# First block of a three-block fp32 kernel: the local projection in four halves between the dilated attention units, the gate sigmoids spread out, the score maxima taken piece by piece

## The reference, cut to what matters

```python
h = rms_norm(x, g_norm1) * (1.0 + sc1) + sh1
proj = h @ w_in
qa, ka, va, qb, kb, vb, gates = jnp.split(proj, split_at, axis=-1)
...
o_a = neighbourhood_attention(qa, ka, va, rpb)          # 8 heads, "local"
for g, (win, dil) in enumerate(DIL_CONFIGS):            # 3 groups of 4 heads, "dilated"
    o_g, lse_g = dilated_window_attention(qb[:, :, sl], kb[:, :, sl], vb[:, :, sl], win, dil)
...
wts = softmax(lse over the three groups);  o_b = sum over g of wts * o_g
gate_a, gate_b = split(sigmoid(gates + b_gate), 2)
merged = gate_a * (o_a @ w_proj_a) + gate_b * (o_b @ w_proj_b)
x = x + gt1 * (merged @ w_o)
```

## Time and profile before

| | us |
|---|---|
| median of 3 runs | 2222.18 (2220.04 to 2225.40) |
| the profiled execution, own time | 2223.02 |
| its span, first to last instruction | 2221.2 |
| PE busy | 2132.8 (96%) |
| DVE busy | 1329.5 (60%) |
| ACT busy | 1148.2 (52%) |
| POOL busy | 86.6 (4%) |
| mean granted TensorE clock | 0.986 of full |

### The profile page before, as it was taken

The page is one execution under the profiler, slowest core; times in us unless marked ns, Lnnn a source line. Parts: engine busy times, 40 slices in busy tenths (PEclk is TensorE's granted clock), DMA queues, the critical chain, the costliest instruction groups (busy, mean ns, idle before and its releaser), DMA issues. The chain is left out here.

```text
span 2221.2 us, 40757 instructions
## 1 busy us (share of the span) xinstructions
PE 2132.8 (96%) x15594; PEld 1865.5 (84%) x15594; DVE 1329.5 (60%) x1821; ACT 1148.2 (52%) x1697; POOL 86.6 (4%) x92
## 2 busy tenths in 40 slices
PE   7999889999999999989999999999999998999998
PEld 5787778887888998888998887887998897998887
DVE  3446375556556987566656555555897575756554
ACT  3454644445445566655445445445557664535444
POOL 1000000000000010100000000000002010000000
PEclk9999999999999999999999999999999999999999
DMA  9763245554553454421455554554354421345553
GB/s 375 279 236 110 77 154 183 187 184 172 189 188 144 179 180 143 154 94 58 171 186 185 188 188 170 189 189 171 136 187 155 163 102 54 137 181 180 189 189 123
DMA packets 53468, 373.16 MB, mean 168 GB/s; under 512 B 6320, under 2 KB 6448, under 8 KB 9424
## 3 DMA queue, kind: packets, MB, share of 16 engines
q1 hardware_dynamic: 47808, 342.00, 42.4%
q0 software_dynamic: 5520, 29.23, 3.8%
HBM read 370.10 MB, written 1.11 MB: 167 GB/s over the span
## 5 line engine op out<-in xcount | busy, mean ns | idle before, releaser
L1507 ACT ACTIVATE HI<-ring 128x1024 fp32r<-128x1024 f32 x606 | 626.3, 1056 | 738.1 <-PE banks L559 397.2
L2067 DVE TENSOR_TENSOR LO<-ring,HI 128x1024 fp32r<-128x1024 f32 x322 | 393.8, 1225 | 369.6 <-ACT HI L1507 369.3
L2073 DVE TENSOR_TENSOR LO<-ring,HI 128x2048 fp32r<-128x2048 f32 x135 | 309.6, 2294 | 242.0 <-ACT HI L1507 242.0
L523 PE MATMUL banks<-UH,HI 128*128 128x256 f32 x1424 | 416.2, 292 | 2.7 <-DVE LO L2073 2.7
L524 PE MATMUL banks<-UL,HI 128*128 128x256 f32 x1424 | 404.2, 284 | 0.0
L525 PE MATMUL banks<-UH,LO 128*128 128x256 f32 x1424 | 404.0, 284 | 0.0
L557 PE MATMUL banks<-HI,UH 128*128 128x512 f32 x896 | 350.2, 391 | 5.6 <-DVE LO L2073 3.5
L559 PE MATMUL banks<-HI,UL 128*128 128x512 f32 x896 | 349.2, 390 | 0.0
L558 PE MATMUL banks<-LO,UH 128*128 128x512 f32 x896 | 349.2, 390 | 0.0
L523 PEld LDWEIGHTS banks<-UH,HI 128*128 128x128 f32 x1424 | 274.3, 193 | 20.1 <-issue 19.0
L524 PEld LDWEIGHTS banks<-UL,HI 128*128 128x128 f32 x1424 | 274.5, 193 | 1.9 <-issue 1.7
(11 more groups left out here) (340 smaller groups left out, 3073.9 us busy)
## 6 DMA issues: line engine op xcount, KB each, us to landing
ring<-in_w_stream SPq DMA_DIRECT2D x315, 1024.0 KB, 4.8
ARENA<-in_ada_stream POOLq DMA_DIRECT2D x16, 1024.0 KB, 6.2
ARENA<-in_ada_stream SPq DMA_DIRECT2D x8, 1024.0 KB, 13.7
GRMS<-cum_rows POOLq DMA_DIRECT2D x16, 256.0 KB, 3.5
ARENA<-in_na_bias POOLq DMA_DIRECT2D x2, 1024.0 KB, 12.7
RMS<-cum_rows POOLq DMA_DIRECT2D x8, 256.0 KB, 3.5
RSTD<-cum_rows POOLq DMA_DIRECT2D x8, 256.0 KB, 3.8
ARENA<-in_ropes POOLq DMA_DIRECT2D x1, 1088.0 KB, 11.2
```

The source lines that it names most:

```text
L523: nc.tensor.matmul(out, lh, rh, start=start, stop=False, **kw)
L1507: nc.scalar.activation(HI[:, q % PARTS, at], ring[:, q % RING, at], ACT.Copy).then_inc(hi_ready, 1)
L2067: nc.vector.tensor_tensor(LO[:, q % PARTS, at], ring[:, q % RING, at], HI[:, q % PARTS, at].bitcast(F32), ALU.subtract).then_inc(lo_ready, 1)
L2073: nc.vector.tensor_tensor(LO[:, q % PARTS, :], ring[:, q % RING, :], HI[:, q % PARTS, :].bitcast(F32), ALU.subtract).then_inc(lo_ready, 2)
```

## The change

1. PE does half (19, 0) before step 0, so steps 0 to 6 hold the seven halves left, steps 7 to 10 the local projection in four halves (`proj_half`, 24 matmuls each, banks 4 and 5 as in the panels before), step 11 `gate_rows(0)`; `gate_rows(1)` follows the last step. Only the dilated projection is left behind it; its tiles 2 and 3 (banks 6 and 7) wait for the rows' copies.
2. ACT copies each projection half out to SBUF (`proj_out`), over the dilated queries, which are used by then. It makes the high parts of panels 25 and 26 in steps 8 and 10, and does the sigmoids in pieces of 5, 3, 3 (steps 9, 10, 11) and 5 (after the last copy of rows).
3. `dil_scale` scales in two parts, first group 0 (2 x 256 columns), then groups 1 and 2 (2 x 512), each with its own count; the turn of group 0 waits for the first only.
4. DVE takes a maximum after each group's scores (512 columns), joins the first two after group 1 (two small instructions), and after group 2 one small instruction gives the negated maximum. `GS` columns 18 to 23 hold the pieces.
5. DVE multiplies by the local gate in SBUF (`near_first`: three in step 11, the fourth after `heads_low(2)`). The low part of panel 20 moves from ahead of the steps to behind the first scores of step 0; that of 21 comes in step 0, 22 in step 3, 23 in step 4, 24 in step 6, 25 and 26 in steps 8 and 10.
6. `WIDE0`, where the later layers' count of `wide_free` begins, goes up by 4.

```diff
@@ PE
+            def proj_half(c):
+                q, w = Q_PROJ1 + c // 2, B1_PANELS + c
+                if c == 0:
+                    pe.wait_ge(otl_ready, 2)
+                src = both(panel(q), lambda x: tiles(x, 4))
+                pe.wait_ge(wide_free, w + 1)
...
+                mm.then_inc(*((proj_done, 1) if c % 2 == 0 else (panel_used, 2)))
...
             b1_half(18, 1)
+            b1_half(19, 0)
             for d in range(DIL_UNITS):
                 for g in range(DIL_GROUPS):
                     k = DIL_GROUPS * d + g
                     turn(NA_UNITS + k)
                     if d + 1 < DIL_UNITS and g < 2:
                         dil_scores(d + 1, 2 * g)
-                    if k < 8:
-                        b1_half(19 + k // 2, k % 2)
-                    elif k == 8:
+                    if k < 7:
+                        b1_half(19 + (k + 1) // 2, (k + 1) % 2)
+                    elif k < 11:
+                        proj_half(k - 7)
+                    else:
                         gate_rows(0, 2 * KT)
-                    elif k == 10:
-                        gate_rows(1, 5 * KT)
                     dil_values(d, g)
...
+            gate_rows(1, 5 * KT)
+            src = both(panel(Q_PROJ1 + 2), lambda x: tiles(x, 2))
             pe.wait_ge(otl_ready, 3)
...
@@ ACT
+            def dil_scale(d):
+                u = NA_UNITS + d
+                act.wait_ge(rden_ready, u + 1)
+                for lo, n in ((0, S), (S, 2 * S)):
+                    for e in range(2):
+                        x = SC[:, d % 2, e * 768 + lo:e * 768 + lo + n]
+                        ins = nc.scalar.activation(x, x, ACT.Copy, scale=RDEN[:, 2 * u + e:2 * u + e + 1])
+                    ins.then_inc(scaled_ready, 1)
...
                     if g == 2 and d + 1 < DIL_UNITS:
-                        softmax_scale(NA_UNITS + d + 1, 768)
-                    if k < 8 and k % 2:
+                        dil_scale(d + 1)
+                    if k < 7 and k % 2 == 0:
                         panel_out(19 + k // 2)
-                    if k == 8:
-                        gate_rows(0)
+                    if 7 <= k < 11:
+                        proj_out(k - 7)
+                    if k in (8, 10):
+                        split(Q_PROJ1 + k // 2 - 4 + PARTS)
+                    if k == 9:
+                        open_gates(0, 5)
                     if k == 10:
-                        gate_rows(1)
+                        open_gates(5, 3)
+                    if k == 11:
+                        open_gates(8, 3)
+            gate_rows(0)
             heads_high(2)
-            for i in range(2 * KT):
...
+            gate_rows(1)
+            open_gates(11, 5)
@@ DVE
                 add.then_inc(scored, 1)
+                dve.wait_ge(scored, u + 1)
+                x = SC[:, d % 2, :].rearrange("p (e g n) -> p e g n", e=2, g=DIL_GROUPS)[:, :, g, :]
+                v = NA_UNITS + d
+                need(step(nc.vector.tensor_reduce(GS[:, 18 + 2 * g:20 + 2 * g], x, AX.X, ALU.max)))
+                if g == 1:
+                    need(step(nc.vector.tensor_tensor(NMAX[:, 2 * v:2 * v + 2], GS[:, 18:20], GS[:, 20:22], ALU.max)))
+                    step(nc.vector.tensor_scalar(NMAX[:, 2 * v:2 * v + 2], NMAX[:, 2 * v:2 * v + 2], -1.0, None, ALU.mult))
                 if g == DIL_GROUPS - 1:
-                    dve.wait_ge(scored, u + 1)
-                    largest(NA_UNITS + d, 768)
+                    c = COLUMNS + 2 * v
+                    nc.vector.scalar_tensor_tensor(NMAX[:, c:c + 2], GS[:, 22:24], -1.0, NMAX[:, 2 * v:2 * v + 2], ALU.mult,
+                                                   ALU.min).then_inc(nmax_ready, 1)
```

More of the change, by code:

```diff
@@ L71 @@
 assert N_PANELS % RING == 0
-WIDE0 = B1_PANELS
+WIDE0 = B1_PANELS + 4
 def columns(sizes):
@@ L183, in build_program @@
         ADA_SUM = region(S)
-        MTMP = ARENA[:, SC_AT:SC_AT + 2048].rearrange("p (t n) -> p t n", t=4)
+        MERGE = PROJ[:, QB:QB + 8, :]
         GROWS = ARENA[:, 0:2 * D].rearrange("p (i n) -> p i n", i=2)
@@ L815, in turn @@
                     d, g = (u - NA_UNITS) // DIL_GROUPS, (u - NA_UNITS) % DIL_GROUPS
-                    pe.wait_ge(scaled_ready, NA_UNITS + d + 1)
+                    pe.wait_ge(scaled_ready, NA_UNITS + 2 * d + (1 if g == 0 else 2))
                     src, at = SC[:, d % 2, :], (g * S, (DIL_GROUPS + g) * S)
@@ L868, in dil_values @@
                 pair_values(u, d // 2 * S + d % 2 * P, (h, h + 1), g == 0, g == DIL_GROUPS - 1)
+            def proj_half(c):
[5 more added lines that the diff above has]
+                for e in range(2):
+                    for k in range(4):
+                        at = c % 2 * S + e * P
+                        mm = product(bank[4 + w % 2][:, e * S:(e + 1) * S], both(src, lambda x: x[:, k, at:at + P]),
+                                     (OTH[:, k, :], OTL[:, k, :]), start=(k == 0), stop=(k == 3))
+                mm.then_inc(*((proj_done, 1) if c % 2 == 0 else (panel_used, 2)))
             def gate_rows(i, at):
@@ L964, in _ @@
                         dil_scores(d + 1, 1)
+            gate_rows(1, 5 * KT)
+            src = both(panel(Q_PROJ1 + 2), lambda x: tiles(x, 2))
             pe.wait_ge(otl_ready, 3)
[L967 to L978, removed]
+            pe.wait_ge(wide_free, 2 + WIDE0)
             for c in range(4):
+                if c == 2:
+                    pe.wait_ge(gate_rows_ready, 4)
                 for e in range(2):
@@ L1671, in softmax_scale, with proj_out, open_gates @@
                 ins.then_inc(scaled_ready, 1)
+            def dil_scale(d):
+                u = NA_UNITS + d
+                act.wait_ge(rden_ready, u + 1)
+                for lo, n in ((0, S), (S, 2 * S)):
+                    for e in range(2):
+                        x = SC[:, d % 2, e * 768 + lo:e * 768 + lo + n]
+                        ins = nc.scalar.activation(x, x, ACT.Copy, scale=RDEN[:, 2 * u + e:2 * u + e + 1])
+                    ins.then_inc(scaled_ready, 1)
+            def proj_out(c):
+                act.wait_ge(*((proj_done, c // 2 + 1) if c % 2 == 0 else (panel_used, 2 * (Q_PROJ1 + c // 2 + 1))))
+                nc.scalar.activation(MERGE[:, 2 * c:2 * c + 2, :], tiles(bank[4 + (B1_PANELS + c) % 2][:, :], 2),
+                                     ACT.Copy).then_inc(wide_free, 1)
+            def open_gates(first, n):
+                act.wait_ge(wide_free, 2 + B1_PANELS)
+                for at in range(first, first + n):
+                    gate = nc.scalar.activation(PROJ[:, GATE + at, :], PROJ[:, GATE + at, :], ACT.Sigmoid, bias=pk1("b_gate", at))
+                if (first + n) % KT == 0:
+                    gate.then_inc(gates_ready, 1)
             def turned(u):
@@ L1711, in _ @@
                     softmax_exp(NA_UNITS, 768)
-                    softmax_scale(NA_UNITS, 768)
+                    dil_scale(0)
             for d in range(DIL_UNITS):
@@ L2309, in heads_low, with near_first @@
                                         OTH[:, 2 * i:2 * i + 2, :].bitcast(F32), ALU.subtract).then_inc(otl_ready, 1)
+            def near_first(c):
+                if c == 0:
+                    dve.wait_ge(gates_ready, 1)
+                dve.wait_ge(wide_free, 2 + B1_PANELS + c + 1)
+                x = MERGE[:, 2 * c:2 * c + 2, :]
+                nc.vector.tensor_tensor(x, x, PROJ[:, GATE + 2 * c:GATE + 2 * c + 2, :], ALU.mult).then_inc(gated_a, 1)
             for q in range(6):
@@ L2360, in _ @@
                             dil_score(d + 1, 0)
+                            if d < 2:
+                                split(18 + 2 * d + PARTS)
                             dil_score(d + 1, 1)
@@ L2364, in _ @@
                             denominators(NA_UNITS + d + 1)
-                    if k < 8 and k % 2:
+                    if k in (0, 4, 6):
                         split(19 + k // 2 + PARTS)
+                    if k in (8, 10):
+                        split(Q_PROJ1 + k // 2 - 4 + PARTS)
+                    if k == 11:
+                        for c in range(3):
+                            near_first(c)
             heads_low(2)
+            near_first(3)
             def merge_first(c, bank_a, gate_a, ta):
@@ L2379, in merge @@
                 nc.vector.tensor_tensor(u, u, tiles(ta, 2), ALU.add).then_inc(merged_ready, 1)
[L2381 to L2387, removed]
+            gate_b = PROJ[:, GATE + 8:GATE + 16, :]
             dve.wait_ge(gates_ready, 2)
@@ L2390, in _ @@
                 if c < 3:
-                    dve.wait_ge(proj_done, c + 1)
+                    dve.wait_ge(proj_done, 2 + c + 1)
                 else:
                     dve.wait_ge(panel_used, 2 * (Q_PROJ1 + B1_PROJ))
-                merge(c, 0, bank[4 + c], gate_b, MTMP[:, c, :])
+                merge(c, 0, bank[4 + c], gate_b, MERGE[:, 2 * c:2 * c + 2, :].rearrange("p t n -> p (t n)"))
                 if c:
```

1 line of the change is left out of this document (removed).

## The result

The changed kernel takes 2206.78 us (median of 5 runs, 2206.16 to 2211.97), the kernel before 2222.18. The ratio is 0.9946 with a 95% interval of 0.9933 to 0.9959: a gain of 12.0 us (9.1 to 14.9), where 11.3 was forecast. The two medians themselves lie 15.4 apart: three of the five runs of the changed kernel took 2206.2 to 2206.8 and two 2211.5 to 2212.0, and the median is one of the three. So 2206.78 lies 4 under the forecast of about 2211 and just under the 2207 at which its range ended. A second set of runs of the same pair gave 0.9955 (0.9940 to 0.9971). The profiled execution took 2211.5 with a span of 2209.7.

A forecast was written before the change was run, and what follows sets the result against it. PE was taken as the bound, busy 96%, so gain comes from its idle time or low clock. 12.0 earlier minus 0.7 for the clock gave 11.3: 2223.0 to 2211.7 profiled, median about 2211, range 2207 to 2217.

The forecast's parts named there:

- The turns: Steps 0 to 9 on PE: step 0 at 206.15, turn 3 at 221.1, turn 6 at 236.0, turn 9 at 251.05.
- Before step 0: Unit 0 on DVE: last addition, its maximum and one small instruction end at 203.05, 0.3 later than in the kernel before.
- ACT as the bound of the tail: Steps 9 to 11: PE waits 0.5, 0.1 and 1.1 for turned weights, 1.65 for the first rows' copies.
- One sign of mine: Profile after: ACT with hardly a hole from the last exponential to the last sigmoid.
- The merge: After the last sigmoids: starts at 271.15, PE starts `w_o` at 274.65; wait for panel 27's low part 2.7 at full clock.
- the clock term: Second rows' spreading on PE, behind new holes of 1.1 and 1.65: 1.95 or 3.27, a loss of 0 to 1.3, taken 0.7.
- The table load: ACT's switch to the sigmoid table ahead of a turned weight: 1.28, no drain; with the skill's drain, 1.4 less gain.
- A: Rival, steps 0 to 9: queues hold up PE more than summed, up to 5.7, gain 5.6, 2216.5; 30%.
- B: Rival, start of `w_o` and after: nothing reaches the end, 2222 or within 4.4 of it; 10%.
- C: Rival, the steps: lower clock stays, each half costs 2.0 more, with all 12 halves 2235; 3%.
- D: Rival, before step 0: half (19, 0) waits for a low part or bank, first hole stays, 3.1 less gain, 2214; 2%.

The follow-up runs named there:

- experiment 2: Changed kernel with half (19, 0) put back behind the first scores of step 0: 2213.16 us, ratio 0.9972 to the kernel before.
- experiment 5: Changed kernel with the scaling in one piece of 2 x 768 columns: 2209.59 us, ratio 0.9955 to the kernel before.
- experiment 4: Changed kernel with one maximum over 1536 columns after the third group: 2210.11 us, ratio 0.9958 to the kernel before.
- experiment 3: Changed kernel with all 16 sigmoids in one piece after the second rows' copy: 2212.19 us, ratio 0.9965 to the kernel before.
- experiment 7: Changed kernel with the last eight sigmoids ahead of the second rows' copy: 2204.01 us, ratio 0.9929 to the kernel before.
- experiment 9: Changed kernel with copies of projection halves and spread rows moved from ACT to DVE: 2204.17 us, ratio 0.9930 to the kernel before.
- experiment 6: Kernel before with only half (19, 0) ahead of step 0 and panels' copies and low parts moved to match: 2217.55 us, ratio 0.9986.

## Why the prediction was right

**The turns.** I forecast step 0 at 206.15, turn 3 at 221.1, turn 6 at 236.0 and turn 9 at 251.05 on the old trace's clock. Measured, and moved to that clock (the table's times plus 190.06): 206.31, 221.06, 235.82, 250.96. Durations read once and summed along each engine's fixed order were enough. That PE is the bound there, so that each microsecond of a hole reaches the turns behind it, is shown by experiments 2 and 5.

**Before step 0.** The exponentials of unit 0 start 13.11 after the first scores instead of 12.67, so 0.4 later where 0.3 was summed; experiment 4 confirms that the pieces cost there.

**ACT as the bound of the tail.** Forecast waits were 0.5, 0.1, 1.1 and 1.65; measured 0.56, 0.26, 1.02 and 1.50. Experiments 3, 7 and 9 show the queue from three sides. One sign of mine did not come: ACT was to have hardly a hole up to the last sigmoid, and it stood 3.29 for the second rows. Some 1.5 of that follows from my own sum (copies done at 266.05, 0.48 for `heads_high(2)`, second rows done at 268.0), the rest is their lower clock.

**The merge.** I had `w_o` at 274.65 plus the clock term of 0.7, so 275.35. Measured 85.90 + 190.06 = 275.96. The wait for panel 27's low part came out at 2.48 for 2.7.

**The clock term is the step that was mis-sized.** I took 0.7, between 0 and 1.3. In this profile the second rows took 3.68 instead of 2.05, 1.6 more and above my upper end, and since ACT waited for them (3.29, experiment 7) and the merge for ACT, all of it reached `w_o`. My upper end of 1.3 was the difference of a partly slow 3.27 to 1.95. A wait is not always paid for so: in the old trace the waits of 1.00 and 0.85 on either side of unit 1 left the clock there at 1.00, and two variants of the changed kernel had the same wait of 1.50 at full clock (last section). Without the loss the stretch would have gained 10.72 + 1.63 = 12.35, where I had 12.0. So a clock term too small by 0.9 and a remainder too small by 0.35 partly cancel, and 10.7 in the stretch stands for 11.3. That cancelling is luck. The runs' 12.0 (9.1 to 14.9) can't tell these values apart.

**The table load** took 1.28 with 0.02 ahead and 0.01 behind it, also now that a turned weight waits for it; in all thirteen profiles the first sigmoid starts 0.01 to 0.02 behind it. The drain of about 1.38 that the Trainium skill, "ScalarE: Activation LUTs", What ACT_TABLE_LOAD costs, adds to it did not show in any of them.

**The rivals.** A, more hold-up by the queues: no wait above 0.6 in steps 0 to 9. B, nothing reaches the end: 10.7 reach the diagonals (125.20 to 114.45). C, the lower clock through the steps: 1.00 in units 0 to 2. D: the half runs where it was put.

**What adds up to the gain.** At one clock, taking back the half ahead costs 4.4, the spread sigmoids 3.5, the scaling in two parts 2.9 and the pieces of the maximum 0.8. That is 11.6 of 12.35, but the parts are not independent (experiment 6), and what the projection halves between the steps are worth by themselves was not run.

## What to carry to other kernels

Work moved into a hole only pays if the place it leaves is filled too: the half ahead of step 0 gave 1.3 us alone and is worth 4.4 inside the whole change. When one engine's in-order queue has become the bound, three things paid here: ordering it by who waits (row copies ahead of sigmoids that are needed last), moving copies to an engine that stands idle, and cutting in two the instruction that the next stage waits for. Compare such stretches from a fixed point inside the trace: here that repeated within 0.15 us, where the runs scatter by 5 to 6.

## What the hardware showed

The clock after a short wait is not the same from profile to profile. The second spreading of rows, 16 matmuls directly behind a wait of 1.50 us (0.7 of work and a wait of 1.02 stand before that), took 3.68, 3.78, 3.68 and 3.58 us in four profiles and 2.05 in two (experiments 2 and 4). Behind waits of 0.30, 0.42, 0.59 and 1.26 us it took 2.05 in all four. The mean granted clock over the 16 matmuls was 0.53 in the changed kernel, near the lower level, and 1.00 in experiment 4. Here are the two cases, each a row of PE's timeline, from experiments 5 and 4:

```profile
264.95 3.68 PE L623 MATMUL banks<-CON,MOD 128*128 128x128 f32 x16 [1.50 <-ACT ARENA L1714]
```

```profile
263.25 2.05 PE L623 MATMUL banks<-CON,MOD 128*128 128x128 f32 x16 [1.50 <-ACT ARENA L1715]
```

So a wait of this length cost its own time and, in four profiles of six, 1.6 us on top. The length of the last wait does not decide it alone. In the kernel before, the last wait ahead of the second rows was 0.80, with 12 small matmuls between, and they took 3.27 and 2.75 in its two profiles:

```profile
258.40 0.66 PE L839 MATMUL banks<-ARENA 128*64 128x128 f32 x8 [0.80 <-ACT ARENA L1677]
258.99 1.02 PE L822 MATMUL banks<-CON,ARENA 128*128 128x128 f32 x4
259.80 3.27 PE L623 MATMUL banks<-CON,MOD 128*128 128x128 f32 x16
```

There waits of 1.66 and 1.00 had come within the 5 us before. That fewer and shorter waits keep the clock up is suggested by these profiles, not shown: what else decides it stays open.
